# Reordered attention steps in three layers of a five-layer transformer kernel: two score chunks side by side, transposes woven into projections, one gate ahead of a normalisation

## What is computed

```python
def _dense_causal(q, k, v, scale, cum=None):       # latent and forget-gate layers
    s = jnp.einsum('bqhd,bkhd->bhqk', q_blk, k) * scale
    if cum_t is not None:                          # forget gate: cumulative log-forget values
        s = s + c_q[..., :, None] - cum_t[:, :, None, :]
    s = jnp.where(k_pos[None, :] <= q_pos[:, None], s, NEG_INF)
    p = jax.nn.softmax(s, axis=-1)
    return jnp.einsum('bhqk,bkhd->bqhd', p, v)

def _swa_branch(x, w_in, sinks, w_out):            # banded: 128 keys back, alibi slopes, sinks
    ...
    p = p / (jnp.sum(p, axis=-1) + jnp.exp(sink - m))
    return (o * jax.nn.silu(gate)) @ w_out

# mixed block: 4 heads that choose 128 keys by an index score, 4 heads of block attention,
# a short convolution and a pooling mixer; then an output projection and a gated MLP
mix = jnp.concatenate([ya, yb, yc, yd], axis=-1) @ w_out[i]
```

## Time and profile before

| | us |
|---|---|
| median of 3 runs | 1652.9 (1652.37 to 1653.56) |
| the profiled execution | 1657.83 |
| its span | 1656.0 |
| PE busy | 1620.8 (98%) |
| DVE, ACT, POOL busy | 776.0, 757.8, 658.2 |

### The profile page before, as it was taken

One profiled execution on the slowest core, in us unless ns is written; L12 is line 12 of the kernel. 1 busy time (PEld: TensorE's weight loads), 2 busy tenths in 40 slices (PEclk: granted clock), 3 DMA queues, 4 the chain that ended last, 5 costly groups with the idle time before them and its releaser, 6 DMA issues.

```text
span 1656.0 us, 26230 instructions
## 1 busy us (share of the span) xinstructions
PE 1620.8 (98%) x10245; PEld 1313.5 (79%) x10245; DVE 776.0 (47%) x2044; ACT 757.8 (46%) x1465; POOL 658.2 (40%) x551
## 2 busy tenths in 40 slices
PE   8999999999999999999999999999999999999998
PEld 7777778887888787788777788777688888888877
DVE  3778635665543434354877464886051111001162
ACT  4566624655345444434576534328553322213252
POOL 5332234332443333243423243882235444444423
PEclk9999999999999999999999998999999999999999
DMA  6323144233452323153312265231243333333412
GB/s 174 71 45 87 52 161 125 80 83 60 160 157 55 85 56 93 58 194 79 88 41 75 73 184 152 79 90 56 90 135 102 102 91 101 102 92 97 120 62 89
DMA packets 216071, 161.32 MB, mean 97 GB/s; under 512 B 53763, under 2 KB 197155, under 8 KB 215948
## 3 DMA queue, kind: packets, MB, share of 16 engines
q1 hardware_dynamic: 205904, 130.21, 28.1%
q10 hardware_dynamic: 9820, 29.40, 5.7%
q0 software_dynamic: 224, 0.03, 0.1%
HBM read 148.32 MB, written 11.14 MB: 96 GB/s over the span
## 4 chain that ended last, share of the span: by engine, by line
PE 80%; DVE 11%; ACT 5%; issue 2%; POOL 2%; DMA 1%; SPq 0%; DVEq 0%; ACTq 0%; POOLq 0%
PE banks L532 40%; PE banks L483 8%; PE banks L485 7%; PE banks L484 7%; PE banks L772 4%; PE banks L716 4%; PE banks L614 4%; PE banks L758 3%; PE banks L738 1%; DVE banks L2354 1%; ACT AB L1512 1%; DVE banks L2343 1%; DVE AB L2356 1%; ACT w_hi L1382 1%; ACT G L1634 1%
## 5 line engine op out<-in xcount | busy, mean ns | idle before, releaser
L2856 POOL TENSOR_TENSOR w_lo<-w_raw,w_hi 128x512 fp32r<-128x512 f32 (+2 forms) x506 | 617.5, 1248 | 968.0 <-ACT w_hi L1382 967.7
L1382 ACT ACTIVATE w_hi<-w_raw 128x1024 fp32r<-128x1024 f32 (+4 forms) x254 | 249.8, 994 | 158.7 <-PE banks L485 102.0
L532 PE MATMUL banks<-XTh,w_hi 128*128 128x512 f32 (+5 forms) x1216 | 283.6, 375 | 7.2 <-DVE XTl L2316 3.0
L532 PE MATMUL banks<-XTl,w_hi 128*128 128x512 f32 (+5 forms) x1216 | 274.0, 367 | 0.0
L532 PE MATMUL banks<-XTh,w_lo 128*128 128x512 f32 (+5 forms) x1216 | 272.4, 367 | 0.0
L532 PEld LDWEIGHTS banks<-XTh,w_hi 128*128 128x128 f32 (+2 forms) x1216 | 209.0, 190 | 53.7 <-issue 8.3
L532 PEld LDWEIGHTS banks<-XTl,w_hi 128*128 128x128 f32 (+2 forms) x1216 | 212.7, 189 | 37.8
L532 PEld LDWEIGHTS banks<-XTh,w_lo 128*128 128x128 f32 (+2 forms) x1216 | 212.7, 189 | 37.4
L483 PE MATMUL banks<-w_hi,OTh 128*128 128x512 f32 (+1 forms) x448 | 172.8, 386 | 1.6 <-DVE QKl L2080 1.5
L484 PE MATMUL banks<-w_lo,OTh 128*128 128x512 f32 (+1 forms) x448 | 167.8, 375 | 0.0
L485 PE MATMUL banks<-w_hi,OTl 128*128 128x512 f32 (+1 forms) x448 | 167.7, 374 | 0.0
(11 more groups left out here) (222 smaller groups left out, 2209.6 us busy)
## 6 DMA issues: line engine op xcount, KB each, us to landing
w_raw<-in_w_gate_up_dram SPq DMA_DIRECT2D x44, 512.0 KB, 3.8
w_raw<-in_fox_w_in_dram SPq DMA_DIRECT2D x30, 512.0 KB, 4.1
w_raw<-in_mla_w_in_dram SPq DMA_DIRECT2D x26, 512.0 KB, 4.9
w_raw<-in_w_in_dram SPq DMA_DIRECT2D x24, 512.0 KB, 4.0
w_raw<-in_w_down_dram SPq DMA_DIRECT2D x22, 512.0 KB, 3.6
w_raw<-in_swa_w_in_dram SPq DMA_DIRECT2D x20, 512.0 KB, 3.8
w_raw<-in_mla_w_out_dram SPq DMA_DIRECT2D x16, 512.0 KB, 3.2
x_spill<-AB ACTq DMA_DIRECT2D x16, 512.0 KB, 2.8
```

Of the source, the lines that this page charges most:

```text
L532: mm = nc.tensor.matmul(o, wt[:, k, :], xt[:, k, lo:hi], start=first and n == 0 and k == 0, stop=last and n == 2 and k == nk - 1, skip_gro ...
L1382: nc.scalar.activation(view(w_hi, u, RING), view(w_raw, u, RAW), ACT.Copy).then_inc(hi_done, 1)
L2856: ins = pool.tensor_tensor(low[at], raw[at], high[at].bitcast(F32), ALU.subtract)
```

## The change

There are three parts. In the forget-gate layer (`aug` is set there) the order of iterations 0 to 5 is now T0, S0, S1, T1 ahead of the projections, and T2 and S2 at the second point of the first projection, after six of its matmuls; S2 is then not issued a second time after the projections. In the mixed block iterations 0 and 1 issue T0 and S0 ahead of the projection, T1 and S1 at its first point and T2 at its third (the old test looked at the first pair, which has no chosen keys, and so was never met); iteration 2 issues T1 and T2 at the first and second point in place of the second and fourth. In the banded layer DVE's iteration 5 computes the gate and the gated output ahead of the second half of the normalisation.

```diff
+                scored = set()
+
                 def step(i, n):
 
+                    if n == 5:
+                        scored.add(i)
                     if n % 2:
                         scores(i + 2, n // 2)
...
                     if i == n_pairs - 2:
-                        return [0], {2: [2], 4: [4]}
+                        return [0], {1: [2], 2: [4]} if pairs[i].sel else {2: [2], 4: [4]}
...
-                    if pairs[0].sel and i >= 0:
+                    if pairs[-1].sel and i >= 0:
                         return [0, 1], {1: [2, 3], 3: [4]}
+                    if pairs[0].aug is not None and 0 <= i < n_pairs - 2:
+                        return [0, 1, 3, 2], {2: [4, 5]}
                     return list(range(5)), {}
...
-                    scores(i + 2, 2)
+                    if i not in scored:
+                        scores(i + 2, 2)
...
-            pair_attention(swa_pairs(), fill, norm_first=(-1,))
+            pair_attention(swa_pairs(), fill, norm_last=(5,), norm_first=(-1,))
```

## The result

The changed kernel takes **1670.4 us** (median of 4 executions, 1669.75 to 1671.24) where the kernel before takes 1652.8: 17.6 us longer, ratio 1.0107, 95% interval 1.0091 to 1.0123. The prediction was 1660.3 with a range up to 1665. It was right that the kernel gets slower; the size and the range were wrong.

A forecast was written before the change was run, and what follows sets the result against it. TensorE, busy 98%, was taken as the bound, so only its waits and low clock count: -0.6 banded + 4.8 forget-gate + 3.2 mixed = +7.4 us, on 1652.9 giving 1660.3 us, range 1651.5 to 1665.

The forecast's parts named there:

- the sum's base: Whole kernel: net +7.4 us added to the profiled 1657.8, then its 4.9 us distance from the median carried over: 1660.3.
- nothing more is lost there: Forget-gate layer: T2 reaches ACT and DVE about 1.4 us later, but their chain has some 3 us of slack.
- Banded layer: Projection of iteration 6: 1.74 us wait for the gate becomes 0.9 to 1.2 ahead of T1; gain 0.6 us.
- Forget-gate layer, S2: Iterations 0 to 5: S2 behind T2 waits 0.94 us for DVE's maxima; layer 4.8 us later in sum.
- waited for nothing: Forget-gate layer: in its old place S2 came after up to three projections and had no wait.
- T2's wait: Forget-gate layer: T2's hidden wait of about 0.2 us for ACT's copy goes in each iteration.
- Mixed block: Iterations 0 to 2: ACT's delayed chain brings three new waits; values' product of iteration 2 starts 3.2 us later.
- the two bounds of 1.7 and 4.9: Mixed block's loss in us: 1.7 with full clock in the product, 4.9 with one more low stretch of the same size.
- by about a microsecond: Mixed block: ACT, not PE, was the later one at T0 of iterations 1 and 2, by this much.
- The rival on this clock: Near 1000 us: the low-clock stretch may vanish as later work shifts, 6.8 us less, 1653.5; chance 0.13.
- The rule on transposes: Forget-gate layer: transposes may not count as busy for the clock, so T1, T2 and a wait could halve it; 9 us more.
- The rival's 1669 us: More low-clock stretches, in the mixed block or by the transpose rule in the forget-gate layer: 1662 to 1669; chance 0.10.

The follow-up runs named there:

- e2: Kernel before with only the forget-gate layer's part of the change; 1660.96 us, ratio 1.0064.
- e1: Kernel before with only the banded layer's part of the change; 1650.72 us against 1652.83, ratio 0.9984.
- e3: Kernel before with only the mixed block's part of the change; 1655.14 us, ratio 1.0021.
- e5: Changed kernel plus ten extra matmuls filling PE's wait at the start of the mixed block; 1662.01 us, ratio to the kernel before 1.0055.
- e6: Kernel before plus ten extra matmuls filling PE's wait at the start of the mixed block; 1652.4 us, ratio 0.9992.
- e9: Kernel before with the forget-gate part, ten extra matmuls, and ACT issuing the forget-gate rows' transfers ahead of the gate's copy; 1656.4 us, ratio 1.0015.
- e4: Kernel before with the forget-gate part, but S2 left in its old place behind the projections; median 1662.25 us, ratio 1.0037.
- e10: Kernel before with ten extra matmuls and only iteration 2 of the mixed block's part; 1650.42 us, ratio 0.9974.
- e8: Kernel before with the forget-gate part, but S2 six matmuls later than T2; executions at 1657.1 to 1657.4 and 1664.1 to 1665.2 us, ratio 1.0056.

## Why the prediction was wrong

Two steps failed. The larger is the sum's base with the clock near 1000 us: the sum put nothing there for the change, and 8.4 us came (the changed kernel takes 1662.0 with the wait filled and 1670.4 without). The other is "nothing more is lost there" in the forget-gate layer: 4.8 us were said and 8.1 came. With the second alone the time would have been 1660.3 + 3.3 = 1663.6, inside the range; the first takes it out.

In numbers of the runs, without the clock near 1000 us: forget-gate layer +8.1 (from e2's trace), banded -0.9 (from e1's trace; its median says -2.1), mixed block +2.3 (e3), sum 9.5 (8.3 with e1's median); e5 against e6, both with the wait filled, is 1662.0 - 1652.4 = 9.6. The clock near 1000 us adds 1670.4 - 1662.0 = 8.4. In the profiles alone, the parts are 8.2 - 0.9 + 4.0, 1.6 for the longer low stretch near 1000 us and 0.4 for a later arrival at the banded layer's end: 13.3 of 13.4.

- **Banded layer**: right. The 1.74 us went, a wait for the normalisation came ahead of T1; gained 0.9 where 0.6 was taken (0.5 to 0.9).
- **Forget-gate layer, S2**: right. A wait of 0.87 us is listed, 0.94 was said; e9, where it is the only new wait, has the layer 4.9 us longer, 4.8 said.
- **Forget-gate layer, "so nothing more is lost there"**: this step failed. The prediction followed the chain from T2 to the next tile's bank, which had 3 us of slack, and took it that S2 "waited for nothing" in its old place. It did not ask what S2 had covered there: the trip of 3.35 to 3.42 us from the gate's copy over the four transfers to S0, which in the kernel before ended just as S0 came. The price is 0.7 us in each of the four iterations without values in between, and e9 took 3.2 us back. The Trainium skill ("DMA: Bandwidth & Descriptors", Anatomy of one DMA — SWDGE (gpsimd) path) puts the fixed cost of a transfer issued from GpSimd at about 2.0 us whatever its size. These are issued from ACT, for which that section gives no figure; here the last 4 KB are issued at 573.57 and S0 starts at 575.45, 1.88 us later, which is near it.
- **T2's wait**: right. 0.2 us were said, and iterations 0 and 3 of e4 are 0.16 us shorter.
- **Mixed block**: right in the new waits, their places and the cause, too high in the sum of waits: 3.2 us were taken and 2.4 came, since the three waits that go (0.87 together) were not counted. The product starts 5.5 us later and not 3.2, because a low stretch now lies ahead of it; at full clock in the product 1.5 of it comes back, and 4.0 remain, between the two bounds of 1.7 and 4.9. Alone the part cost 2.3. That ACT was the later one "by about a microsecond" is misread: the 1.34 and 0.91 us run from the start of T0 to ACT's copy, and 0.68 of that passes where ACT is free, too, so ACT was late by 0.66 and 0.23. What the prediction did not see is that iteration 2 alone is a gain (e10).
- **The sum's base**: this step failed. The prediction carried "the difference over" from the profiled execution, 4.9 us above the median, as if both had the same clock. That execution had the low stretch near 1000 us, as by their mean clock 17 of the 85 others had, and the median had not. The rival on this clock was seen only from one side, as 6.8 us that might be gained; for most executions there was nothing to gain, but 8 us to lose. Put on that side, it gives 1652.8 + 7.4 + 8.4 = 1668.6.
- **The rule on transposes**: the clock in the forget-gate layer stayed at 1.00 from 560 to 708 us, with T1, T2 and a wait close together. The rival's 1669 us is near the result by chance; its place was wrong. Near 1000 us the transposes are the same with and without the filled wait, and the kernel with the filled wait kept its clock, so they are not enough to take it down.

What stays open is why all four executions of the changed kernel fell near 1000 us while of e2, which reaches that place about as late, two of six did. By the mean clock, the fall is in 20 of the 109 executions with the old forget-gate layer (the kernel before, e1, e3) and in 16 of the 26 with a changed one (e2, e4, e8, the changed kernel). The parts of the change that come ahead of that place only shift it in time. That filling the wait cures it is shown; what in the shift brings it on is not.

## What to carry to other kernels

When a step is taken from its place, ask not only what it waits for in the new place but what it hid in the old one: measure from the last thing issued before it to the next instruction that depends on another engine or a transfer, and see whether that trip is as long as what stood in it. Before a profiled execution is used as the base of a sum, compare its time and granted clock with those of the other executions; where they differ, name the stretch, and price its coming as well as its going. A weave that delays the first copy of a long chain on another engine can pay for it two iterations later, even if the wait that it was meant for gets shorter.

## What was not expected of the hardware

A wait of 1.20 us followed by narrow matmuls and transposes could take PE down to 1.2 GHz, and it stayed there for all 48 matmuls of 128 columns that follow, and for some of the 256 columns behind them. In the kernel before, eight matmuls of 128 columns take 0.89 us from start to start at full clock (998.11 to 999.00) and 1.71 at half (1002.80 to 1004.51). By their times and mean clocks, the same kernel did this in 17 of 85 executions, at 5 to 8 us each. Ten useless matmuls ahead of the wait removed it from all 74 executions of the seven kernels that had them, and cost nothing that could be measured (e6: ratio 0.9992). The Trainium skill ("TensorE: Matmul & The Clock Gate", HAM oscillation — how this bites in real kernels) tells of idle time of PE, there waits for transfers, as what brings the clock down again and again; here the wait that was filled was one for DVE, and the clock fell behind it only in some executions.
